# Narrow w2 products of the experts issued for two groups at a time, and a reordered program head, in a two-block transformer kernel

## What is computed

```python
cond = jax.nn.silu(c)
for l in range(DEPTH):
    mod = cond @ w_mod[l] + b_mod[l]
    sh1, sc1, g1, sh2, sc2, g2 = jnp.split(mod, 6, axis=-1)
    h = _modulate(_rmsnorm(x, norm1_w[l]), sh1, sc1)
    x = x + g1 * _mixer(h, ...)
    h = _modulate(_rmsnorm(x, norm2_w[l]), sh2, sc2)
    y = _swiglu(h, ffn_w1, ffn_w3, ffn_w2) if l % 2 == 0 else _moe(h, ...)
    x = x + g2 * y

def _moe(h, router_w, router_b, w1, w3, w2):
    # each token goes to its two best experts, weighted
    out = sum(combine[..., e:e+1] * (silu(h @ w1[e]) * (h @ w3[e])) @ w2[e] for e in range(8))
```

## Time and profile before

| what | value |
|---|---|
| median of three runs | 2364.27 us |
| the profiled execution | 2359.99 us |
| its span (first to last instruction) | 2358.2 us |
| PE busy | 2289.7 us (97%) |
| PEld busy | 1799.4 us (76%) |
| DVE / ACT busy | 847.7 us (36%) / 462.8 us (20%) |
| bytes moved | 538.05 MB, 228 GB/s over the span |
| mean granted TensorE clock | 0.996 of full |

### The profile page before, as it was taken

The page is one execution under the profiler, slowest core; times in us unless marked ns, Lnnn a source line. Parts: engine busy times, 40 slices in busy tenths (PEclk is TensorE's granted clock), DMA queues, the critical chain, the costliest instruction groups (busy, mean ns, idle before and its releaser), DMA issues.

```text
span 2358.2 us, 49861 instructions
## 1 busy us (share of the span) xinstructions
PE 2289.7 (97%) x22244; PEld 1799.4 (76%) x22244; DVE 847.7 (36%) x1819; ACT 462.8 (20%) x853; POOL 27.0 (1%) x64
## 2 busy tenths in 40 slices
PE   7999999999999999999999999999999999999998
PEld 6888767777688877777777777777768867888884
DVE  3675652665435562321011010110123442343443
ACT  2343311000125331200000000000013331232332
POOL 2000000000000000000000000000000000000000
PEclk9999999999999999999999999999999999999999
DMA  9453255776443424569999999999963323333310
GB/s 369 180 215 142 90 221 190 284 285 277 169 143 126 143 98 151 215 265 383 396 369 394 385 380 391 379 395 397 400 252 108 109 106 143 125 110 132 117 72 19
DMA packets 75531, 538.05 MB, mean 228 GB/s; under 512 B 8552, under 2 KB 8560, under 8 KB 11440
## 3 DMA queue, kind: packets, MB, share of 16 engines
q1 hardware_dynamic: 72864, 526.14, 58.4%
q0 software_dynamic: 1360, 4.85, 0.6%
q10 hardware_dynamic: 1088, 3.81, 0.4%
HBM read 529.90 MB, written 4.85 MB: 227 GB/s over the span
## 4 chain that ended last, share of the span: by engine, by line
PE 92%; DVE 4%; ACT 2%; issue 1%; POOL 1%; DVEq 0%; ACTq 0%; POOLq 0%
PE ps L905 20%; PE ps L471 16%; PE ps L427 14%; PE ps L438 11%; PE ps L924 7%; PE ps L928 4%; PE ps L739 3%; PE ps L859 3%; PE ps L764 2%; PE ps L514 2%; PE ps L1078 2%; PE ps L1032 1%; PE ps L1048 1%; DVE ring L1788 1%; ACT ring L1411 1%
## 5 line engine op out<-in xcount | busy, mean ns | idle before, releaser
L905 PEld LDWEIGHTS ps<-hT,ring 128*64 128x64 f32 x11264 | 470.8, 137 | 43.3 <-issue 39.0
L905 PE MATMUL ps<-hT,ring 128*64 128x96 f32 x11264 | 487.4, 247 | 9.2 <-issue 5.0
L471 PE MATMUL ps<-ring,hT 128*128 128x256 f32 x1792 | 401.0, 380 | 2.7 <-DVE hT L1788 2.1
L471 PEld LDWEIGHTS ps<-ring,hT 128*128 128x128 f32 x1792 | 335.4, 190 | 52.3 <-issue 5.0
L427 PE MATMUL ps<-ring,hT 128*128 128x256 f32 x1664 | 366.1, 380 | 0.0
L427 PEld LDWEIGHTS ps<-ring,hT 128*128 128x128 f32 x1664 | 314.1, 190 | 44.6 <-issue 2.5
L1411 ACT ACTIVATE RA<-ps 128x192 f32<-128x192 f32 (+2 forms) x159 | 69.8, 439 | 1145.0 <-PE ps L905 609.7
L1788 DVE TENSOR_TENSOR RA<-ps,RA 128x192 f32<-128x192 f32 (+1 forms) x99 | 39.1, 395 | 698.7 <-PE ps L905 615.4
L438 PE MATMUL ps<-hT,ring 128*128 128x256 f32 (+1 forms) x1280 | 269.0, 370 | 0.1
L438 PEld LDWEIGHTS ps<-hT,ring 128*128 128x128 f32 x1280 | 232.0, 190 | 33.1 <-issue 3.1
L924 PE MATMUL ps<-ring,RA 128*64 128x512 f32 x704 | 167.6, 595 | 0.9 <-issue 0.9
(11 more groups left out here) (299 smaller groups left out, 1695.7 us busy)
## 6 DMA issues: line engine op xcount, KB each, us to landing
ring<-stream SPq DMA_DIRECT2D x497, 1024.0 KB, 6.9
slots_scratch<-YT ACTq DMA_DIRECT2D x7, 384.0 KB, 7.5
x_rows<-x SPq DMA_DIRECT2D x2, 512.0 KB, 8.2
gates_row<-bgate SPq DMA_DIRECT2D x1, 1024.0 KB, 9.0
QT<-bgate SPq DMA_DIRECT2D x1, 1024.0 KB, 11.0
rows_scratch<-RB ACTq DMA_DIRECT2D x2, 512.0 KB, 4.5
out<-x_rows SPq DMA_DIRECT2D x2, 512.0 KB, 2.6
rowt<-rows SPq DMA_DIRECT2D x1, 460.0 KB, 7.3
```

The costliest lines, as they stand in the source:

```text
L471: m = pe.matmul(ps[:, b, t * UC:(t + 1) * UC], hT[:, k, t * P:(t + 1) * P], ring[:, s, k * UC:(k + 1) * UC], start=k == 0, stop=k == KC - 1)
L905: m = pe.matmul(ps[64 * j:64 * (j + 1), b, c * CAP:(c + 1) * CAP], ring[:, s, k * UC + c * P + 64 * j:k * UC + c * P + 64 * (j + 1)], hT[: ...
```

## The change

In the experts, `expert_down` no longer issues the narrow products (last 32 slots) of every group. For an even group it issues only the wide products and keeps group and slot in a list; for the next, odd group it issues that group's wide products and then the narrow products of both groups. The last group, 10, is alone. `actT_e` gets a third buffer. The ring slot of an even group's w2 unit is released four `unit_done` counts of the odd group later, and `ring_plan` says so to SP. `slot_tokens` uses two column tiles of 64 where one of 96 was, over 128 slots.

In the head, x is loaded after unit 7. GpSimd signals `ident_made` as soon as `ident` is there, and `masks_made` is waited for later. VectorE does the units before `norm_rows`, and sums `lead_part(1)` and `lead_part(2)` one behind the other.

```diff
-EXPERT_INCS = FG * sum(INCS.values())
+DOWN_PAIRS = (FG + 1) // 2
+EXPERT_INCS = FG * (INCS["w1m"] + INCS["w3m"]) + DOWN_PAIRS * INCS["w2m"]
...
-        freed[who] += INCS.get(name, 1)
-        last[s] = (len(out) - 1, who, freed[who])
+        first_of_pair = name == "w2m" and j % 2 == 0 and j < FG - 1
+        freed[who] += 0 if first_of_pair else INCS.get(name, 1)
+        last[s] = (len(out) - 1, who, freed[who] + (sum(INCS.values()) if first_of_pair else 0))
...
-        actT_e = RA[:, 1, 1024:1024 + 4 * CAP].rearrange("p (n k s) -> p n k s", n=2, k=2)
+        actT_e = RA[:, 1, 1024:1024 + 6 * CAP].rearrange("p (n k s) -> p n k s", n=3, k=2)
...
                 if l == 0:
                     pe.wait_ge(*from_dve.more())
+                    pe.wait_ge(ident_made, 1)
                     mod(l, range(8))
                     lead_spread(len(LEAD) - 1)
-                    pe.wait_ge(masks_made, 1)
                     norm_turn("n10", 0)
...
                 for j in range(2, 5):
                     rows_unit("act", ("a", l, j))
+                if l == 0:
+                    pe.wait_ge(masks_made, 1)
                 diff_attention(l)
...
-                    m = pe.matmul(ps[0:CAP, b, 0:2], pick[:, t, 0:CAP], tokw[:, t, :],
-                                  start=t == 0, stop=t == T - 1)
-                finish(m, "dve", [b], key)
+                    ms = [pe.matmul(ps[o:o + WIDE, b, 0:2], pick[:, t, o:o + WIDE], tokw[:, t, :],
+                                    start=t == 0, stop=t == T - 1) for o in range(0, P, WIDE)]
+                finish(ms, "dve", [b], key)
...
                 for k in range(2):
                     for j in range(2):
-                        pe.matmul(ps[64 * j:64 * (j + 1), 4, :], actT_e[:, g % 2, k, 0:WIDE],
-                                  ring[:, s, k * D + 512 * j:k * D + 512 * (j + 1)], **flags[k])
-                for k in range(2):
-                    for j in range(4):
-                        m = pe.matmul(ps[32 * j:32 * (j + 1), 5, 0:256], actT_e[:, g % 2, k, WIDE:CAP],
-                                      ring[:, s, k * D + 256 * j:k * D + 256 * (j + 1)], **flags[k])
-                        if k:
-                            m.then_inc(unit_done, 1)
-                            done.more()
+                        pe.matmul(ps[64 * j:64 * (j + 1), 4, :], actT_e[:, g % 3, k, 0:WIDE],
+                                  ring[:, s, k * D + 512 * j:k * D + 512 * (j + 1)], **flags(g, k))
+                kept.append((g, s))
+                if g % 2 == 0 and g < FG - 1:
+                    return
+                for g_, s_ in kept:
+                    for k in range(2):
+                        for j in range(4):
+                            m = pe.matmul(ps[32 * j:32 * (j + 1), 5, 0:256], actT_e[:, g_ % 3, k, WIDE:CAP],
+                                          ring[:, s_, k * D + 256 * j:k * D + 256 * (j + 1)], **flags(g_, k))
+                            if k and g_ == g:
+                                m.then_inc(unit_done, 1)
+                                done.more()
+                kept.clear()
...
-                if u == 2:
+                if u == 8:
                     for t in range(T):
                         sp.dma_start(x[:, t, :], x_d[t * P:(t + 1) * P, :]).then_inc(x_in[t], 16)
...
+            link(pool.memset(pool_note[:, :], 0.0))
+            pool.memset(junk[:, :], 0.0).then_inc(ident_made, 1)
...
-                            lead_part(LEAD.index(j))
+                        if j == LEAD[1]:
+                            for i in (1, 2):
+                                lead_part(i)
...
+                    dve.wait_ge(ident_made, 1)
                     lead_part(0)
+                    mod(l, range(8))
                     for t in range(T):
                         dve.wait_ge(x_in[t], 16)
                         norm_rows(t)
-                    dve.wait_ge(masks_made, 1)
-                    mod(l, range(8))
                     lead_out(len(LEAD) - 1)
                     mod_bias(l, 0, A1_l[l], "n1")
```

More of the change, by code:

```diff
@@ L219, in two_blocks @@
         junk_a = sb("junk_a", P, 1)
+        pool_note = sb("pool_note", P, 1)
         small = sb("small", P, 512)
@@ L283, in two_blocks @@
         masks_made = sem("masks_made")
+        ident_made = sem("ident_made")
         eps_made = sem("eps_made")
@@ L296, in two_blocks @@
         last = stages.index(stop) if stop else len(stages) - 1
[L299 removed]
+        gain = {unit_done: EXPERT_INCS, burst_for_dve: 4,
                 act_took: FG, dve_took: FG + 4, dve_gave_pe: 1, dve_step: 20,
@@ L912, in expert_unit @@
                 taken_by(who, [b], key)
+            kept = []
             def expert_down(l, g, turn):
@@ L920, in expert_down, with flags @@
                     free(5)
-                flags = [dict(start=g == 0 and k == 0, stop=g == FG - 1 and k == 1) for k in range(2)]
+                def flags(g, k):
+                    return dict(start=g == 0 and k == 0, stop=g == FG - 1 and k == 1)
                 for k in range(2):
                     for j in range(2):
-                        pe.matmul(ps[64 * j:64 * (j + 1), 4, :], actT_e[:, g % 2, k, 0:WIDE],
-                                  ring[:, s, k * D + 512 * j:k * D + 512 * (j + 1)], **flags[k])
-                for k in range(2):
-                    for j in range(4):
-                        m = pe.matmul(ps[32 * j:32 * (j + 1), 5, 0:256], actT_e[:, g % 2, k, WIDE:CAP],
-                                      ring[:, s, k * D + 256 * j:k * D + 256 * (j + 1)], **flags[k])
-                        if k:
-                            m.then_inc(unit_done, 1)
-                            done.more()
+                        pe.matmul(ps[64 * j:64 * (j + 1), 4, :], actT_e[:, g % 3, k, 0:WIDE],
[12 more added lines that the diff above has]
+                kept.clear()
                 full["y", l, 1] = (4, unit_done, done.n)
@@ L1359, in _ @@
                                     base=0, pattern=[[1, NE], [-1, NE]], channel_multiplier=0))
-            pool.memset(junk[:, :], 0.0).then_inc(masks_made, 1)
+            pool.memset(pool_note[:, :], 0.0).then_inc(masks_made, 1)
             def token_gather(l):
@@ L2235, in mixer @@
                         norm_out("n10", t, A1_l[0], modc_l[0][:, 0:8])
+                    dve.wait_ge(masks_made, 1)
                     constants()
@@ L2260, in hidden @@
                     else:
-                        tt(actT_e[:, g % 2, :, :], view(b, 2, CAP), gate_e[:, g % 2, :, :], ALU.mult, c=took)
+                        tt(actT_e[:, g % 3, :, :], view(b, 2, CAP), gate_e[:, g % 2, :, :], ALU.mult, c=took)
                     if dense and g == 0:
```

2 lines of the change are left out of this document (1 added, 1 removed).

## The result

The changed kernel takes 2342.39 us (median of four, 2339.7 to 2346.28) where the kernel before takes 2364.73 (median of four, 2362.37 to 2365.24): a ratio of 0.9909, interval 0.989 to 0.9927, or 22.3 us less. Forecast were 2347.2 and a range of 2343.5 to 2355. A second sample of the changed kernel gave 0.9905 (0.9886 to 0.9924).

The account below looks back on a forecast made before the run. TensorE was taken to bound the kernel nearly throughout. From the profiled 2359.99 us, 11.4 (visits), 2.4 (token matmuls) and 3.3 (head) came off, giving 2342.9; plus 4.3 for the median, 2347.2, range 2343.5 to 2355.

Parts of the forecast that it names:

- the 17.1 us of the sum: Whole kernel: total saving forecast, 11.4 for narrow-tile visits, 2.4 for token matmuls and 3.3 for the head.
- the clock fall in the head: Head, idle stretch before the first projection: the granted clock falls and loses 1.7 us, bounds 0 and 3.4.
- The signs of being right: Next profile: wide run to L905 1.72 to 1.75 us, eight token records 0.25, L471 at 33.8, no 4 us diagonal wait.
- Visits to the narrow tiles: Experts on TensorE: 40 fewer visits at 0.285 us save 11.4 us; going from L924 straight to L905 costs 0.
- Token matmuls: Experts, seven times: eight records in their neighbours' tiles take 0.24 us instead of 0.59, saving 2.4 us.
- The later release costs 0, and the waits on "issue" stay: Experts: holding an even w2 slot 8 us longer fits memory, cost 0; no term for TensorE's eight unexplained waits, 5.0 us.
- the reasoning by units ahead: Experts: eleven slots are some 29 us of TensorE; the first delayed load has about 19 us left before it is read.
- a rival on the slow side: Experts: load bursts hold up instruction packets, one 0.63 us wait per pair of groups, 25 us, giving 2372; chance 0.05.
- Head: First projection starts 5.0 us earlier, less 1.7 for the clock: saves 3.3 us (1.6 to 5.0).
- The followed schedule: Head: unit-by-unit timeline of TensorE and VectorE, starting L471 at 33.8 to 33.9 us instead of 38.84.
- The median of the runs lies 4.3 above it: Whole kernel: 4.3 us added to the profiled execution's forecast of 2342.9, giving 2347.2 for the median.
- its lower end: Whole kernel, 2343.5 us: a clock that never falls (-1.7) and a few unexplained waits gone (-2).

Follow-up runs that it names:

- Triples: The changed kernel with the narrow products of three groups issued together and four activation buffers: 2336.51 us, ratio 0.9892 to the kernel before.
- `tok_only`: The kernel before with only the token matmuls put in two column tiles of 64, with 128-wide comparisons: median 2363.14 us, ratio 0.999.
- `head_only`: The kernel before with only the head's changes (early ident_made, x after unit 7, units summed back to back, norm rows last): median 2360.31 us, ratio 0.9984.

## Why the prediction was wrong

The step that failed is the 17.1 us of the sum, in two of its terms. The gain from the later release and from fewer waits on "issue" was put at nothing, and the clock fall in the head was priced too high. The signs of being right (the rows, the 1.72, the first projection near 33.8) came out, but none of them asks whether the waits become fewer or what a short fall of the clock costs.

- **Visits to the narrow tiles:** right. Forecast 0.285 us each and 11.4 in all with nothing for the new change of line; measured 0.28 to 0.29, and four plain steps of 0.43 ahead of L911. Triples agreed with the price. The rule of the Trainium skill that the prediction cites ("TensorEngine Tiling (Array Packing)", section Tiling Modes: a change of the tiling mode drains TensorE) agrees with the 1.72 us, where the mode stays.
- **Token matmuls:** right by the timeline, 2.5 for 2.4; the time of `tok_only` gives 1.2 +- 0.8.
- **The later release costs 0, and the waits on "issue" stay:** this failed. The later release did cost nothing, and the reasoning by units ahead foretold where it breaks. But it gained, 2.3, 2.3 and 3.3 us in the three samples with the order of before, and that was in no term; the waits appeared only as a rival on the slow side and as 2 us in the range. In the first two profiles they went from 5.9 to 3.5 us, and the experts gained 16.5 where the two terms make 14.1 (11.6 + 2.5). Over more profiles it is more: the experts took 739.5, 741.5 and 739.4 us in the two profiles of before and in `head_only`, and 723.0, 718.1, 721.5, 722.9 and 719.8 in the five with all parts of the change, 19 us less in the mean, 5 more than 14.1; their waits on "issue" fell from 5.8 to 2.3 us in the mean. The later release alone gives 2.3 to 3.3 of these 5, and the rest is not explained.
- **Head:** mis-sized, 3.3 for a measured 4.4 to 4.5. The price of the clock fall, 1.7, was 0.7 in the profile and 0.6 to 2.2 over eight profiles, 1.1 in the mean. The followed schedule met L475 at 33.63 for a forecast of 33.8 with some luck: it took over unit 0's 6.60 us from one profile, and the seven profiles with the new order, x behind unit 7 and no fill start the projection between 31.98 and 33.85.
- **"The median of the runs lies 4.3 above it":** not where the forecast failed. Adding the 4.3 only means taking the 17.1 off the median of before (2364.3 - 17.1 = 2347.2), which was sound. The change is worth more than 17.1: 22.3 between medians, 22.3 at equal clock in the second sample, 21.2 as the sum of its parts. That the two profiled executions differ by 17.5, near the forecast, is luck: the clock was low for 23.9 us ahead of the last microseconds in the one after and for 17.1 in the one before, and the 3.4 us this cost behind the experts hid what the sum lacked.
- **Range:** its lower end allowed 1.7 for the clock and 2 for the waits, 3.7 in all. The head's 1.1 and the experts' 2.7 (16.5 for 13.8) use up 3.8. The last 1.0 us down to 2342.39 is within the interval of the measurement, which reaches from 17.3 to 26.0 us less than before.

## What to carry to other kernels

Where small column tiles alternate with larger ones, count the entries and exits (0.29 us for one visit here) and gather the small products, as far as the ring allows: count the units still ahead when the first held slot comes free, and keep their time above the time to landing; two groups held ran without a wait for a load, three nearly so, four cost 76 us. When several terms of a wait chain are rearranged, ask which one moved: here the early signal for `ident` gave most of the head's gain, the late x the rest, and the sums back to back 0.1 us. Take a forecast off the median of the runs, and do not judge it by the difference of two single profiled executions; read the granted clock of both first. And give a term to waits that nothing explains: the change can make them fewer as well as more.

## What the runs showed of the hardware

- A change between the 64-wide and the 32-wide column tiles costs on both sides (0.09 and 0.15 us, with 0.05 in the first run behind), one between different products of the same tiling nothing measurable: 1.72 us for four steps of 0.43.
- The same program shows different clock falls from execution to execution at the same place: 1.00 and 0.76 in 364 to 378 us. In fits over the runs of five kernels, with mean clocks of 0.992 to 0.997, each 0.001 of mean clock goes with 1.4 to 2.9 us.
- The first load of the stream let TensorE start at 6.24 to 7.56 us in these profiles. Its matmul records then start 0.43 us apart and, from 9.1 to 12.7 us on, 0.22 apart, from the point where the trace records the full clock. With the new head and x loaded late the third unit ended between 18.12 and 20.34 us; with the old head, behind GpSimd's wait, it started between 21.56 and 21.70 us in all.
- Loads issued six at a time instead of one by one, the median landing 11.0 instead of 7.5 us after issue, made TensorE no slower and the kernel 3.3 +- 0.7 us faster at equal clock.
- From 1020 to 1645 us, in 16 profiles, all 54 waits of TensorE of more than 0.15 us that no engine and no load explains end 1.2 to 1.6 us after the end of a 16 KB instruction packet. There are 29 of them in the four profiles where ring loads are issued one by one and 25 in the twelve where they are issued in bursts.
